# Gates and projections of a block's merge computed with features on the partitions, and wide attention units' maxima ahead of the scaling

## What is computed

```
(qa, ka, va, iq, ik, iw, qr, kr, vr, gr, ga, gb) = split(h @ w_in)
y_a = att @ w_attn_proj                                   # 512 -> 1024
y_r = (silu(gr) * _head_groupnorm(ret, gn_w)) @ w_ret_proj  # 1024 -> 1024
merged = sigmoid(ga) * y_a + sigmoid(gb) * y_r
x = x + gate1 * (merged @ w_out)
h2 = _rmsnorm(x, norm2_w) * (1.0 + scale2) + shift2
ffn = (silu(h2 @ w_ffn_gate) * (h2 @ w_ffn_up)) @ w_ffn_down
```

## Time and profile before

| | |
|---|---|
| Median of 3 executions | 1582.07 us (1581.46 to 1583.87) |
| The profiled execution | 1581.52 us, span 1579.7 us |
| Granted clock of TensorE, mean | 0.997 of full |
| TensorE busy with matmuls | 1553.5 us, 98% of the span |
| TensorE loading weights (overlaps) | 1256.6 us, 80% |
| Vector busy | 871.2 us, 55% |
| Scalar busy | 606.5 us, 38% |
| GpSimd busy | 44.7 us, 3% |
| DMA | 165.75 MB, mean 105 GB/s |

### The profile page before, as it was taken

How to read it: one execution, slowest core, us unless ns; L and a number is a source line. 1 busy time by engine, 2 the same in 40 slices (tenths; PEclk the granted TensorE clock), 3 DMA queues, 4 the chain that set the end, 5 groups by cost and what they waited for, 6 DMA issues and landing times.

```text
span 1579.7 us, 19715 instructions
## 1 busy us (share of the span) xinstructions
PE 1553.5 (98%) x8019; PEld 1256.6 (80%) x8019; DVE 871.2 (55%) x1581; ACT 606.5 (38%) x1038; POOL 44.7 (3%) x82
## 2 busy tenths in 40 slices
PE   7999999999999999999999999999999999999999
PEld 5777888788888888888888886776778888888887
DVE  6679786655375743332233575676466555555432
ACT  4443334542312432222232354656425433434330
POOL 0000000000000000000000011100010000000000
PEclk9999999999999999999999999999999999999999
DMA  9323122146355244222232143110113233222311
GB/s 386 132 79 102 52 69 67 54 168 219 107 173 173 95 146 160 94 93 91 96 107 93 41 141 113 44 41 15 54 54 134 80 107 107 94 81 92 119 69 54
DMA packets 44882, 165.75 MB, mean 105 GB/s; under 512 B 5108, under 2 KB 5236, under 8 KB 43640
## 3 DMA queue, kind: packets, MB, share of 16 engines
q1 hardware_dynamic: 44792, 164.50, 30.1%
HBM read 162.38 MB, written 2.10 MB: 104 GB/s over the span
## 4 chain that ended last, share of the span: by engine, by line
PE 91%; DVE 5%; ACT 2%; issue 1%; POOL 0%; DMA 0%; SPq 0%; DVEq 0%; ACTq 0%
PE bank L547 87%; PE bank L556 4%; DVE AR L1712 1%; DVE wl L1700 1%; ACT AR L1369 0%; DVE AR L2022 0%; DVE G L1719 0%; DVE X L1712 0%; DVE Hl L1712 0%; ACT wh L1194 0%; POOL ST L2516 0%; ACT AR L1217 0%; DVE ST L1712 0%; DVE CST L1712 0%; DMA CST<-in_cst 0%
## 5 line engine op out<-in xcount | busy, mean ns | idle before, releaser
L547 PE MATMUL bank<-wh,Hh 128*128 128x512 f32 (+1 forms) x1008 | 406.9, 404 | 1.9 <-DVE Hl L1712 1.0
L547 PE MATMUL bank<-wh,Hl 128*128 128x512 f32 (+1 forms) x1008 | 391.8, 389 | 0.0
L547 PE MATMUL bank<-wl,Hh 128*128 128x512 f32 (+1 forms) x1008 | 391.3, 388 | 0.0
L1194 ACT ACTIVATE wh<-raw 128x1024 fp32r<-128x1024 f32 (+1 forms) x195 | 203.7, 1048 | 395.9 <-PE bank L547 383.5
L1700 DVE TENSOR_TENSOR wl<-raw,wh 128x1024 fp32r<-128x1024 f32 (+1 forms) x195 | 234.1, 1208 | 143.4 <-ACT wh L1194 142.5
L547 PEld LDWEIGHTS bank<-wh,Hh 128*128 128x128 f32 x1008 | 189.7, 188 | 58.6 <-issue 22.7
L547 PEld LDWEIGHTS bank<-wh,Hl 128*128 128x128 f32 x1008 | 189.8, 188 | 39.9
L547 PEld LDWEIGHTS bank<-wl,Hh 128*128 128x128 f32 x1008 | 190.2, 189 | 34.2
L547 PE MATMUL bank<-Hh,wh 128*128 128x512 f32 (+2 forms) x504 | 190.1, 377 | 1.0 <-DVE AR L1712 0.7
L547 PE MATMUL bank<-Hl,wh 128*128 128x512 f32 (+2 forms) x504 | 189.3, 376 | 0.0
L547 PE MATMUL bank<-Hh,wl 128*128 128x512 f32 (+2 forms) x504 | 189.3, 376 | 0.0
(11 more groups left out here) (248 smaller groups left out, 1815.2 us busy)
## 6 DMA issues: line engine op xcount, KB each, us to landing
raw<-in_wst SPq DMA_DIRECT2D x268, 512.0 KB, 3.6
AR<-in_wst SPq DMA_DIRECT2D x8, 1024.0 KB, 10.8
X<-in_x SPq DMA_DIRECT2D x8, 512.0 KB, 4.7
AR<-in_wst SPq DMA_DIRECT2D x5, 512.0 KB, 6.2
out<-X SPq DMA_DIRECT2D x8, 256.0 KB, 2.1
CST<-in_cst SPq DMA_DIRECT2D x1, 1619.0 KB, 11.1
raw<-in_wst SPq DMA_DIRECT2D x4, 296.0 KB, 2.8
BC<-in_bc SPq DMA_DIRECT2D x2, 512.0 KB, 8.9
```

The lines of the kernel that those rows point to most:

```text
L547: return e.matmul(o, l, r, start=start, stop=stop, skip_group_check=True)
L1194: e.activation(HI[slot[i]][:, 0:width(i)], raw[:, i % NR, 0:width(i)], ACT.Copy).then_inc(*w_hi.mark(i))
```

## The change

- From ga0 to rp1 the operands swap places (`flip`): a 128x128 tile of the weights is stationary, all 512 tokens of a feature tile are moving, and the products have output features on the partitions. The loop variable t now counts output feature tiles of the half. `sga` and `sgb` hold eight feature tiles of 512 tokens.
- The merged values then lie as wo0 and wo1 want them. Their turns on TensorE go; Scalar copies each feature tile from `sga` to its high part and Vector subtracts: tiles 0 to 3 into Ah and Al during rp0 and rp1's start, tiles 4 to 7 into Hh and Hl when rp1 is over. wo0 and wo1 wait for each feature tile by itself.
- Since gb1 reads all of Hh to its end, the turns of Y go from gb1 to ap0 and ap1, before steps 2, 4, 6 and 8 after gb1, and the row and column sums come at steps 4 and 6 of gb1. ap0 and rp0 wait for all token tiles of their input.
- Ah and Al serve as extra weight buffers only from `up` on.
- Vector does a wide unit's maxima before the scaling of the unit before it, in both attentions; narrow units keep the order.
- In 2nq, the scaling of query tiles 2 and 3 comes 4 steps behind their end (10 and 12 before), the fold of tile 3 2 steps behind (4 before), and the turn and the copy of both 7 steps behind (13 and 14 before).

```diff
-        if k and name == "wo0" and ticks[k - 1][0] == "rp1":
-            avail += [(v, place["ap1", 1]) for v in (NH, NH + 1)]
+        if k and name == "up" and ticks[k - 1][0] == "wo1":
+            avail += [(v, place["wo1", 1]) for v in (NH, NH + 1)]
...
-                while avail and avail[0][0] >= NH and not (place["wo0", 0] <= at < place["2kv", 0] or at >= place["2up0", 0]):
+                while avail and avail[0][0] >= NH and not (place["up0", 0] <= at < place["2kv", 0] or at >= place["2up0", 0]):
...
+            def part(x, h, l, q, t, flip, b, start, stop):
+
+                if flip:
+                    return mm3(b, (h[:, q, tok(t)], l[:, q, tok(t)]), x, start, stop)
+                return mm3(b, x, (h[:, q, :], l[:, q, :]), start, stop)
...
+            WIDE = lambda k, t: (Hh[:, k, :], Hl[:, k, :])
+            AWIDE = lambda k, t: (Ah[:, k, :], Al[:, k, :])
...
+            w.after(4, lambda: row_sum(2, (6, 7)))
+            w.after(6, lambda: column_sum(3, 6))
+            by_tile("gb1", ["gb1"], 8, WIDE, H1, lambda t, n: act.of(("gb1", t)), flip=True)
+            for t in range(T):
+                w.after(2 + 2 * t, lambda t=t: turn_rows(t))
             for n in (0, 1):
-                tokens(f"ap{n}", 4, 512, AHL, lambda t: dve.of(("a1", "out", t)), lambda t, n=n: dve.of((f"ap{n}", t)))
+                tokens(f"ap{n}", 4, 512, AWIDE, lambda t: dve.of(("a1", "out", T - 1)), lambda t, n=n: dve.of((f"ap{n}", t)), flip=True)
...
-            by_tile("rp1", ["rp1"], 8, H, HY, lambda t, n: dve.of(("rp1", t)),
-                    pairs("m", lambda t, n: sga[:, t, 512 * n:512 * n + 512], lambda t, n: dve.of((f"m{n}", t))))
-            HM = lambda t: dve.of(("m", "low", t, 1))
+            HY = lambda t: dve.of(("y", "low", T - 1, 1))
+            tokens("rp0", 8, 512, WIDE, HY, lambda t: dve.of(("rp0", t)), flip=True)
+            by_tile("rp1", ["rp1"], 8, WIDE, HY, lambda t, n: dve.of(("rp1", t)), flip=True)
+
+            def merged(k, t):
+                on.wait_ge(*dve.of(("m", "low", k)))
+                return AHL(k, t) if k < 4 else H(k, t)
...
-                    lambda t: w.after((8, 9, 13, 14)[t], lambda: turn_heads("nq", t, 2, TN[t], dve.of(("nq", "roped", t)))), 2)
+                    lambda t: w.after((8, 9, 7, 7)[t], lambda: turn_heads("nq", t, 2, TN[t], dve.of(("nq", "roped", t)))), 2)
...
+            def merged_high(*ks):
+
+                for k in ks:
+                    on.wait_ge(*dve.of(("m", k)))
+                    on.wait_ge(*(dense.of(("ap1", T - 1)) if k < 4 else dense.of(("rp1", T - 1, 0))))
+                    e.activation((Ah if k < 4 else Hh)[:, k, :], sga[:, k, :], ACT.Copy).then_inc(*act.mark(("m", "high", k)))
+
+            for j, t in w.steps("rp0"):
+                if j == 3:
+                    w.after(2, lambda t=t: merged_high(t))
             for t, n, j in w.steps("rp1"):
-                if j == 3:
-                    w.after(2, lambda t=t: pairs("m", t, dense.of(("rp1", t, 0))))
+                if (t, j) == (T - 1, 3):
+                    w.after(1, lambda: merged_high(4, 5))
+                    w.after(2, lambda: merged_high(6, 7))
...
+
+                    wide = u < n and len(a.units[u][1]) > 1
+                    if wide:
+                        scores(u)
                     if 1 <= u < n + 1:
                         scale(u - 1)
-                    if u < n:
+                    if u < n and not wide:
                         scores(u)
...
+            def merged_low(*ks):
+                for k in ks:
+                    h, l = (Ah, Al) if k < 4 else (Hh, Hl)
+                    on.wait_ge(*act.of(("m", "high", k)))
+                    tt(l[:, k, :], sga[:, k, :], h[:, k, :].bitcast(f32), SUB, ("m", "low", k))
 
             for j, t in w.steps("rp0"):
                 if j == 3:
                     merge(0, t, ("rp0", t))
+                    w.after(3, lambda t=t: merged_low(t))
             for t, n, j in w.steps("rp1"):
                 if j == 3:
                     merge(1, t, ("rp1", t, 0))
-                    w.after(2, lambda t=t: pairs("m", t))
+                    if t == T - 1:
+                        w.after(2, lambda: merged_low(4, 5))
+                        w.after(3, lambda: merged_low(6, 7))
...
-                    w.after((2, 2, 2, 4)[t], root)
-                    w.after((4, 6, 10, 12)[t], scale)
+                    w.after(2, root)
+                    w.after((4, 6, 4, 4)[t], scale)
```

More of the change, by code:

```diff
@@ L860, in turn_pair @@
                 free[b] = dve.of((name, "low", t, n))
-            def pairs(name, src, ready):
-                def both(t):
-                    for n in (0, 1):
-                        turn_pair(name, t, n, src(t, n), ready(t, n), 4 + (2 * t + n) % 4)
-                return lambda t: w.after(2, lambda: both(t))
-            by_tile("gb1", ["gb1"], 8, H, H1, lambda t, n: act.of(("gb1", t)),
-                    pairs("y", lambda t, n: Y[:, t, 512 * n:512 * n + 512], lambda t, n: dve.of((f"y{n}", t))))
@@ L882, in tensor_program @@
-            by_tile("wo1", ["wo1"], 8, H, HM, lambda t, n: dve.of(("wo1", t)), lambda t: w.after(4, lambda: norm_turn("n2", t)))
+            by_tile("wo0", ["wo0"], 8, merged, HM, lambda t, n: dve.of(("wo0", t)))
+            by_tile("wo1", ["wo1"], 8, merged, HM, lambda t, n: dve.of(("wo1", t)), lambda t: w.after(4, lambda: norm_turn("n2", t)))
             def up(prefix, tag, freed, fourth=None):
@@ L1412, in scalar_program @@
                     on.wait_ge(*dense.of(("ga0", t, 0)))
-                    e.activation(sga[:, t, 0:512], bank[t % 2][:, :], ACT.Sigmoid).then_inc(*act.mark(("ga0", t)))
+                    e.activation(sga[:, t, :], bank[t % 2][:, :], ACT.Sigmoid).then_inc(*act.mark(("ga0", t)))
             for key, n, dst in (("ga1", 1, sga), ("gb0", 0, sgb)):
@@ L1431, in scalar_program, with rows_high @@
                     on.wait_ge(*dense.of(("gb1", t, 0)))
-                    e.activation(sgb[:, t, 512:1024], bank[t][:, :], ACT.Sigmoid).then_inc(*act.mark(("gb1", t)))
-                    w.after(2, lambda t=t: pairs("y", t, dense.of(("gb1", t, 0))))
+                    e.activation(sgb[:, 4 + t, :], bank[t][:, :], ACT.Sigmoid).then_inc(*act.mark(("gb1", t)))
+            def rows_high(t):
+                for n in (0, 1):
+                    pair_high("y", t, n, 4 + (2 * t + n) % 4, 4 * n, dense.of(("gb1", T - 1, 0)))
+            for t in range(T):
+                w.after(2 + 2 * t, lambda t=t: rows_high(t))
             for key in ("ap0", "ap1"):
@@ L1437, in scalar_program @@
             w.settle()
-            for _ in w.steps("rp0"):
-                pass
+            def merged_high(*ks):
[6 more added lines that the diff above has]
+                    w.after(2, lambda t=t: merged_high(t))
             for t, n, j in w.steps("rp1"):
-                if j == 3:
-                    w.after(2, lambda t=t: pairs("m", t, dense.of(("rp1", t, 0))))
+                if (t, j) == (T - 1, 3):
+                    w.after(1, lambda: merged_high(4, 5))
+                    w.after(2, lambda: merged_high(6, 7))
             for _ in w.steps("wo0"):
@@ L2087, in pair_low, with rows_low @@
                 tt(Hl[:, k0:k0 + 4, tok(t)], bank[b][:, :].rearrange("p (j q) -> p j q", j=4), ho.bitcast(f32), SUB, (name, "low", t, n))
-            def pairs(name, t):
-                for n in (0, 1):
-                    pair_low(name, t, n, 4 + (2 * t + n) % 4, 4 * n)
-            for t, n, j in w.steps("gb1"):
-                if j == 3:
-                    w.after(2, lambda t=t: pairs("y", t))
-            w.after(2, lambda: take_rows(2, (6, 7)))
-            w.after(4, lambda: take_columns(3, MC[:, 16:24], 6))
+            w.after(4, lambda: take_rows(2, (6, 7)))
+            w.after(6, lambda: take_columns(3, MC[:, 16:24], 6))
+            for _ in w.steps("gb1"):
+                pass
+            def rows_low(t):
+                for n in (0, 1):
+                    pair_low("y", t, n, 4 + (2 * t + n) % 4, 4 * n)
+            for t in range(T):
+                w.after(2 + 2 * t, lambda t=t: rows_low(t))
             for n in (0, 1):
@@ L2100, in vector_program @@
                     if j == 1:
[L2101 removed]
+                        s = sga[:, 4 * n + t, :]
                         on.wait_ge(*dense.of((f"ap{n}", t)))
```

41 lines of the change are left out of this document (18 added, 23 removed).

## The result

| | before | after |
|---|---|---|
| median (range) | 1582.65 us (1581.46 to 1583.87, 5 executions) | 1574.66 us (1571.98 to 1575.66, 5 executions) |
| profiled execution / its span | 1581.5 / 1579.7 us | 1572.0 / 1570.2 us |
| mean granted clock, profiled | 0.997 | 1.000 (the other four: 0.998) |

The ratio is 0.9946, 95% interval 0.9934 to 0.9957: 8.0 us less. The forecast was 13.6 us less, 1568.4, and its range of 1565.8 to 1573.6 missed the median by 1.1 us. The profiled executions differ by 9.5 us. Two gaps are thus to be explained: 4.1 us between the forecast for the profiled execution (1567.9) and what it took, and 2.7 us between that execution and the median.

The account below looks back on a forecast made before the run. TensorE, busy 98% of the span, was taken as the bound. 3.5 (turns) + 11.2 (second attention) - 0.7 - 0.2 - 0.2 = 13.6 us less: 1567.9 profiled, 1568.4 as median, range 1565.8 to 1573.6.

Parts of the forecast that it names:

- Flipped products: ga0 to rp1: 672 matmuls with swapped operands keep 0.227 us each; no difference, 0.7 us to either side.
- Turns removed: Merged rows: four pairs of turn groups leave TensorE, 0.87 us each, 3.5 us won.
- (a): End of rp0: three subtractions delay rp1's last weight chunk on Vector; wait of 0.1 to 0.2 us, bounds 0 and 0.7.
- (c): Ah and Al lent later: three chunks converted at up's start; 0.2 us wait for last norm half, bounds 0 and 2.4.
- (b): Tiles 4 to 7 split after rp1, in time for wo0; no wait, cover 1.9 us, bounds 0 and 1.5.
- R3: Rival, chance 0.09: the wait moves to the merge, (a), (b) or up's start at upper ends; 1572.6 us.
- Place A: First compressed scores, second attention: loss 4.25 us with clock; a 0.7 us wait remains, 3.5 won.
- R2: Rival, chance 0.14: Vector bounds the second attention; displaced scaling or late GpSimd root leaves Place A whole, perhaps B; 1572.8.
- B: Second compressed scores: 0.84 us wait at 1024.74 goes, since the maxima start when the scores are there.
- C: Transposes needing bank 2, second attention: 3.24 us wait until 1042.90 and 2.9 us clock loss go, 6.1 in all.
- R1: Rival, chance 0.12: TensorE's clock doesn't come back after small waits in Place A, perhaps C; 1570 to 1573 us.
- The signs: Expected in the trace: wo0 3.5 us earlier, 0.227 us matmuls, under 1 us before first compressed scores, clock 1.00 throughout second attention.

Follow-up runs that it names:

- e1: Kernel before with only the planner's edit (fifth and sixth weight buffers lent from the first FFN's up stage on): 1587.88 us, ratio 1.0011.
- e9: Changed kernel with only the fourth weight chunk of the second key/value stage held back one step: median 1572.55 us, ratio 0.9927.
- e2: Changed kernel with the third and fourth weight chunks of the second key/value stage split at the old steps: median 1570.32 us, ratio 0.9902.
- e6: Kernel before with only the earlier steps (sum, scaling, turn) of query tiles 2 and 3: median 1575.78 us, ratio 0.9947.
- e10: Changed kernel with late key/value chunks and early compressed-keys copy, but wide units' maxima behind the scaling again: median 1572.52 us, ratio 0.9916.
- e12: Changed kernel with both key/value chunks late and the compressed-keys copy one step earlier, run again: median 1569.44 us, ratio 0.9902.
- a0: Changed kernel run once more, unedited, beside the kernel before on another chip: median 1574.59 us, ratio 0.9940.
- e3: Changed kernel with Vector's copy of the compressed keys out of bank 2 one step earlier: median 1570.96 us, ratio 0.9905.
- e5: Changed kernel with the second attention as before, so the merge and its planner alone: median 1584.01 us, ratio 0.9997 to before.
- e13: Changed kernel with twelve unread transposes on TensorE in the wait ahead of the first projection: median 1572.72 us, ratio 0.9937.
- e14: Changed kernel with late key/value chunks, early compressed-keys copy and twelve unread transposes at the start: median 1567.04 us, ratio 0.9904.
- e15: Changed kernel with late key/value chunks, early compressed-keys copy and twenty-four unread transposes at the start: median 1568.52 us, ratio 0.9910.

## Where the prediction was right and where it failed

**Flipped products, right.** In rp1 of the changed kernel, eleven flipped matmuls (first and last) start 2.27 us apart, as in the earlier trace rows:

```profile
469.67 0.39 PE L548 MATMUL bank<-Hh,wh 128*128 128x512 f32 x1
...
471.94 0.39 PE L548 MATMUL bank<-Hl,wh 128*128 128x512 f32 x1
```

**Turns removed, right.** 3.5 less the waits (a) and (c) was to leave 3.1 us; 3.2 were there at wo0 and still at 894, with no new wait in rp1, wo0, wo1 or up, so (a), (b) and what was seen of (c) cost nothing, and if all of it is the turns', a pair was worth 0.81 rather than 0.87. The Trainium skill's figure ("TensorE: Matmul & The Clock Gate", Back-to-back issue gap) made 2.6 of it; the trace doesn't agree.

**Term (c), the step that failed: -2.3 us.** The prediction weighed what the later joining of Ah and Al does in wo0, wo1 and up's first steps. It took the steady state behind that to be the same and didn't follow the planner's list to the stage where the two buffers leave it. The wait at 914 takes 2.3 of 3.2 us (shown by e1, where the list alone brings it, and by e9 and e2, which take it away by halves). It is R3 in kind, the merge's gain lost to a wait, but neither at (a) nor (b) nor up's start.

**Place A, undersized: 0.7 us of remaining wait was forecast, 1.79 + 0.36 = 2.15 measured: -1.45 us.** The prediction followed the maxima and never asked who holds bank 2 when tile 2's turn is moved ahead of the first scores. It had counted that turn, at 0.35 us (it takes 0.56, from 1005.64 to the next matmul at 1006.20), and had even put "a small copy" behind tile 3's scaling; it didn't ask who waits for that copy. Its reason for the gain, maxima ahead of the scaling, wasn't what brought it: the same two waits stand in e6 without the new order. Of the runs, only those with the copy early show it at work (e10 against e12). R2 named a displaced scaling as the cause of a whole A; it was that, through the copy behind it.

**B and C, right in size; B in part by luck.** 0.84 and 3.24 us of waits went. C went as foretold, by the query tile's earlier steps (e6). B went by them too, and not by the maxima that the prediction gave as the reason. In the profiled execution the clock's losses behind A and C are gone, where the earlier trace rows had 0.56 to 0.80:

```profile
1003.00:1010.00 7.00, 4.84 (x43) 3.53 (x42) 4.93 (x28) 4.73 (x24) 0.00 (x0) 1.00 0.15 59
1010.00:1018.00 8.00, 8.00 (x54) 6.48 (x52) 5.56 (x20) 6.66 (x24) 0.00 (x0) 1.00 0.01 2
1018.00:1050.00 32.00, 32.00 (x275) 24.55 (x274) 25.90 (x86) 20.19 (x53) 0.00 (x0) 1.00 0.10 34
```

**The sum.** 13.6 + 0.1 (the merge's 3.2 for 3.1) - 2.3 - 1.45 = 9.95; the profiled executions differ by 9.5. Of the last 0.45 us, 0.3 are missing at 1039.68 already, without a name; the rest is a wait further on, before and after:

```profile
1216.09 0.39 PE L547 MATMUL bank<-Hh,Ah 128*128 128x256 f32 x1 [0.49 <-DVE X L1712]
```
```profile
1206.58 0.39 PE L548 MATMUL bank<-Hh,Ah 128*128 128x256 f32 x1 [0.66 <-DVE X L1737]
```

**From the profile to the median: -1.6 us.** The prediction added 0.55, the distance of the profiled execution of before to the median of the runs shown. For five executions of before the distance is 1.1 us, for the changed kernel 2.7, since its profiled execution was the one in five at 1.000. 9.5 - (2.7 - 1.1) = 7.9, against 8.0 measured. So R1, the clock that doesn't come back in places A and C, was wrong there: it did come back. The median pays for falls elsewhere: at 19 us, which no part of the change touches (a0), and, as e3, e5 and e13 let one expect, in some executions behind the new wait at 914.

**The signs.** Nearly every sign that the prediction listed came true: the flipped matmuls at 0.227, under 1 us ahead of the first compressed scores, none near the second and third, the clock at 1.00. wo0 begins 3.2 us earlier, not 3.5. The losses lay where it had set no sign: behind up, and at the turn of query tile 2.

## What to carry to other kernels

When an edit changes when a resource enters a rotating list, compute the plan to the end of the kernel and compare each step, because the effect shows where the resource leaves the list. When an operation is moved ahead, list every resource that it claims (here a bank) with the holder of that moment and the place of the holder's release in its own engine's order. And a forecast for a median needs the spread: compare executions at the same mean granted clock, and look for the stretch in which the others lose theirs.

## What was new about the hardware

**A single wait of about 2 us makes TensorE's clock fall in some executions and not in others.** (The six whole falls at the start aren't counted here, since two waits stand close together there.) Behind the wait of 2.1 us at 914 it fell in three profiles of six, for 1.6 us of loss; behind that of 1.79 us it fell in none of seven; behind those of 2.25 to 2.56 us at the first compressed scores in all five, and behind the 3.24 us of place C in all four. One of the three at 914 (e3: length, busy times, granted clock as above):

```profile
915.00:919.00 4.00, 4.00 (x13) 3.15 (x12) 3.02 (x5) 2.73 (x6) 0.81 (x3) 0.63 0.01 4
```

Kernels alike up to there do both (the two profiles of the changed kernel keep the clock at 914, that of e3 doesn't), so the time has steps of some 1.6 to 3.2 us from one execution to the next. The mean granted clock of an execution tells that there was a fall, not where. A fall was seen with no long wait ahead of it, too: in e6 behind the column sum at 503, whose sixteen matmuls have one column each, for 1.6 us. The Trainium skill ("TensorE: Matmul & The Clock Gate", What's actually happening) says that what the chip counts for its clock isn't in step with the kernel, so that the point of a change varies; that agrees with these profiles.

**The clock can, it seems, be held by work that nobody reads.** Twelve 128x128 turns, 1.53 us, stood in a wait of 1 to 2 us at the start, and all five executions of e14 kept a mean of 1.000, where five of nine without them didn't. No profile caught twelve in the case with the DMA's wait; twenty-four, 2.84 us, held the clock in the one that did, and cost 1.5 us more than twelve by the medians (e15 against e14).
